# Scores of the local attention from high and low parts of queries and keys, in three float32r products

## The reference, cut to what matters

```python
def swa_sink_mixer(h, w_in, b_in, sinks, w_out, b_out):
    proj = h @ w_in + b_in
    q, k, v = jnp.split(proj, [...], axis=-1)
    ...
    s = jnp.einsum('bnqkgd,bnskd->bnkgqs', q, kb) * (SWA_HEAD_DIM ** -0.5)
    ...
    mx = jnp.maximum(jnp.max(s, axis=-1, keepdims=True), sink)
    e = jnp.exp(s - mx)
    p = e / (jnp.sum(e, axis=-1, keepdims=True) + jnp.exp(sink - mx))
    o = jnp.einsum('bnkgqs,bnskd->bnqkgd', p.astype(vb.dtype), vb)
    return o.reshape(B, T, SWA_Q_HEADS * SWA_HEAD_DIM) @ w_out + b_out
```

## Time and profile before

| | us |
|---|---|
| median of three runs | 1897.83 (1897.42 to 1898.5) |
| the profiled execution's own time | 1897.43 |
| its span in the profile | 1895.6 |
| TensorE busy, of the span | 1888.5 |
| VectorE busy | 1344.0 |
| ScalarE busy | 987.4 |
| full float32 score matmuls of the local attention | 128 instructions, first at 586.0, last at 651.5 |

### The profile page before, as it was taken

The page is one execution under the profiler, slowest core; times in us unless marked ns, Lnnn a source line. Parts: engine busy times, 40 slices in busy tenths (PEclk is TensorE's granted clock), DMA queues, the critical chain, the costliest instruction groups (busy, mean ns, idle before and its releaser), DMA issues. The chain is left out here.

```text
span 1895.6 us, 25342 instructions
## 1 busy us (share of the span) xinstructions
PE 1888.5 (100%) x9432; PEld 1554.5 (82%) x9432; DVE 1344.0 (71%) x2000; ACT 987.4 (52%) x1591; POOL 96.1 (5%) x114
## 2 busy tenths in 40 slices
PE   9999999999999999999999999999999999999999
PEld 8877888888888788888888988667788888888887
DVE  8656665556566766665666788998897877767867
ACT  5634464454546756454544335788435455545454
POOL 0100000101000000000100000000000000100101
PEclk9999999999999999999999999999999999999999
DMA  7632156758323124766742346232234634654735
GB/s 232 157 100 100 66 152 174 168 161 216 119 67 143 45 67 131 192 147 176 178 154 68 122 134 170 87 94 73 90 96 138 167 89 156 157 149 116 199 96 122
DMA packets 70684, 249.79 MB, mean 132 GB/s; under 512 B 7970, under 2 KB 8226, under 8 KB 69924
## 3 DMA queue, kind: packets, MB, share of 16 engines
q1 hardware_dynamic: 56448, 198.82, 31.2%
q0 software_dynamic: 13824, 49.29, 15.1%
q10 hardware_dynamic: 292, 0.07, 0.0%
HBM read 246.05 MB, written 2.10 MB: 131 GB/s over the span
## 5 line engine op out<-in xcount | busy, mean ns | idle before, releaser
L553 PE MATMUL ps<-HH,WH 128*128 128x512 f32 (+1 forms) x1676 | 623.4, 372 | 0.0
L555 PE MATMUL ps<-HH,WL 128*128 128x512 f32 (+1 forms) x1676 | 618.4, 369 | 0.0
L554 PE MATMUL ps<-HL,WH 128*128 128x512 f32 (+1 forms) x1676 | 618.2, 369 | 0.0
L1346 ACT ACTIVATE WH<-WR 128x1024 fp32r<-128x1024 f32 x331 | 346.9, 1056 | 473.3 <-PE ps L555 308.9
L2109 DVE TENSOR_TENSOR WL<-WR,WH 128x1024 fp32r<-128x1024 f32 x330 | 400.7, 1219 | 260.0 <-ACT WH L1346 259.3
L553 PEld LDWEIGHTS ps<-HH,WH 128*128 128x128 f32 x1676 | 316.2, 189 | 62.3 <-issue 10.0
L555 PEld LDWEIGHTS ps<-HH,WL 128*128 128x128 f32 x1676 | 316.2, 189 | 53.0
L554 PEld LDWEIGHTS ps<-HL,WH 128*128 128x128 f32 x1676 | 316.3, 189 | 51.2
L1006 PE MATMUL ps<-WL,AH 128*128 128x512 f32 x490 | 190.9, 390 | 0.0
L1005 PE MATMUL ps<-WH,AL 128*128 128x512 f32 x490 | 190.8, 389 | 0.0
L1004 PE MATMUL ps<-WH,AH 128*128 128x512 f32 x490 | 190.8, 389 | 0.0
(11 more groups left out here) (401 smaller groups left out, 2616.0 us busy)
## 6 DMA issues: line engine op xcount, KB each, us to landing
WR<-in_up SPq DMA_DIRECT2D x96, 512.0 KB, 4.4
WR<-in_quart SPq DMA_DIRECT2D x60, 512.0 KB, 3.5
WR<-in_quart POOLq DMA_DIRECT2D x48, 512.0 KB, 6.4
WR<-in_in SPq DMA_DIRECT2D x48, 512.0 KB, 3.5
WR<-in_down SPq DMA_DIRECT2D x16, 512.0 KB, 3.5
WR<-in_quartf SPq DMA_DIRECT2D x14, 512.0 KB, 3.5
WR<-in_quartf POOLq DMA_DIRECT2D x14, 512.0 KB, 5.7
MT<-in_up SPq DMA_DIRECT2D x12, 512.0 KB, 3.8
```

The lines of the kernel that those rows point to most:

```text
L553: e.matmul(ps, wh, hi[:, c, cols], start=c == 0 and not (shared and h), stop=False, skip_group_check=shared)
L554: e.matmul(ps, wh, lo[:, c, cols], start=False, stop=False, skip_group_check=shared)
L555: y = e.matmul(ps, wl, hi[:, c, cols], start=False, stop=c == x.n - 1, skip_group_check=shared)
L1346: e.activation(x.wh[:, 0:n], raw(m, x.raw)[:, 0:n], AF.Copy).then_inc(*k.mark("whi", u))
```

## The change

The scores are no longer one product of `WQ` and `WK` in full float32. ScalarE copies keys and each query pair to float32r (`WKH`, `WQH`, the latter with two buffers), VectorE subtracts these from the float32 values (`WKL`, and `WQL`, which lie over `WK` and `WQ`), and TensorE adds three float32r products in PSUM for each block and head: high query x high key, high query x low key, low query x high key. `score(p)` waits for the low parts instead of the evacuations.

```diff
     def score(p):
-        e.wait_ge(*k.on("ae", u + 2 + p))
-        e.wait_ge(*k.on("ae", u))
+        e.wait_ge(*k.on("hlo", "q", p))
+        e.wait_ge(*k.on("hlo", "k"))
+        qh, ql = m.WQH[:, p % 2, :], m.WQL[:, p, :]
...
-                for s in range(2):
-                    b, half = SWA_BANKS[g][s], slice(64 * s, 64 * s + 64)
-                    x = e.matmul(ps[b][:, f:f + n], m.WQ[half, p, blk * 128:(blk + 1) * 128], m.WK[half, k0:k0 + n],
-                                 start=True, stop=True)
+                for j, (query, key) in enumerate(((qh, m.WKH), (qh, m.WKL), (ql, m.WKH))):
+                    for s in range(2):
+                        b, half = SWA_BANKS[g][s], slice(64 * s, 64 * s + 64)
+                        x = e.matmul(ps[b][:, f:f + n], query[half, blk * 128:(blk + 1) * 128], key[half, k0:k0 + n],
+                                     start=j == 0, stop=j == 2)
...
     def evac(j):      # ScalarE
         if j == 0:
             e.activation(m.WK[:, :], p, AF.Identity, bias=par(m, "swa_bk")).then_inc(*k.mark("ae", u + j))
+            e.wait_ge(*k.on("ae", u + j))
+            e.activation(m.WKH[:, :], m.WK[:, :], AF.Copy).then_inc(*k.mark("hhi", "k"))
...
+            e.wait_ge(*k.on("ae", u + j))
+            if j > 3:
+                e.wait_ge(*k.on("score", "w", 2 * j - 7, 1))
+            e.activation(m.WQH[:, j % 2, :], m.WQ[:, j - 2, :], AF.Copy).then_inc(*k.mark("hhi", "q", j - 2))
...
+    def low_q(p):     # VectorE
+        e.wait_ge(*k.on("hhi", "q", p))
+        e.tensor_tensor(m.WQL[:, p, :], m.WQ[:, p, :], m.WQH[:, p % 2, :].bitcast(F32), A.subtract).then_inc(
+            *k.mark("hlo", "q", p))
+
     for j in range(1, 5):
         v_cut(e, k, u + j + 3)
+        if j == 1:
+            e.wait_ge(*k.on("hhi", "k"))
+            e.tensor_tensor(m.WKL[:, :], m.WK[:, :], m.WKH[:, :].bitcast(F32), A.subtract).then_inc(*k.mark("hlo", "k"))
+        elif j > 2:
+            low_q(j - 3)
     for p in range(8):
         score(2 * p)
         score(2 * p + 1)
...
         weigh(2 * p + 1)
+        if p < 6:
+            low_q(p + 2)
```

More of the change, by code:

```diff
@@ L341, in memory @@
     m.WQ = arena("WQ", [128, 8, T], 0)
+    m.WQL = arena("WQL", [128, 8, T], 0, F32R)
+    m.WKL = over("WKL", [128, T], acc, F32R)
+    m.WKH = over("WKH", [128, T], dg + 2 * KB, F32R)
+    m.WQH = over("WQH", [128, 2, T], tmp, F32R)
     m.PW = arena("PW", [128, 4, 896], 16)
@@ L1072, in score @@
                 k0, n = SWA_KEYS[blk]
-                for s in range(2):
-                    b, half = SWA_BANKS[g][s], slice(64 * s, 64 * s + 64)
-                    x = e.matmul(ps[b][:, f:f + n], m.WQ[half, p, blk * 128:(blk + 1) * 128], m.WK[half, k0:k0 + n],
-                                 start=True, stop=True)
-                    if blk == group[-1]:
-                        x.then_inc(*k.mark("score", "w", 2 * p + s, g))
-                        k.free[b] = ("smax", "w", 2 * p + s, g)
+                for j, (query, key) in enumerate(((qh, m.WKH), (qh, m.WKL), (ql, m.WKH))):
[3 more added lines that the diff above has]
+                                     start=j == 0, stop=j == 2)
+                        if blk == group[-1] and j == 2:
+                            x.then_inc(*k.mark("score", "w", 2 * p + s, g))
+                            k.free[b] = ("smax", "w", 2 * p + s, g)
                 f += n
```

## The result

The changed kernel takes 1900.5 us, median of 22 runs (1899.3 to 1902.6); the kernel before 1897.6 (22 runs, 1897.2 to 1898.5). The ratio is 1.0015, interval 1.0009 to 1.0021: 2.9 us slower, a small but measured loss. The prediction was 1899.8 in 1896.8 to 1902.5, no change leaning to slower. The scatter is part of the result. Sorted by the mean TensorE clock of the whole execution, the 22 runs are two groups: eleven from 1899.3 to 1900.3 with a clock of 1.000, and eleven from 1900.7 to 1902.6 with 0.999 or 0.998. The median of the first group is 2.3 us above before, that of the second 3.8. The times alone leave only 0.3 us between the groups, so it is the clock that divides them. The profiled execution, 1901.25 around a span of 1899.4, is one of the second.

What follows compares the result with a forecast made beforehand. TensorE, busy 1888.5 of 1895.6 us, was taken as the bound, with waits at out(0) and out(5) deciding. Terms +1.84 - 0.33 + 0.595 gave +2.1 us, so 1899.8 us, range 1896.8 to 1902.5.

Steps and rivals of the forecast that it cites:

- TensorE's own work: Score calls: 1.62 us against 1.72, about 0.11 less per call, 0.9 us for all eight.
- B: Rival in the score calls: float32r halves don't run side by side; +8.7 us, 1906.5; chance 0.13.
- C: Rival in the score calls: 128 columns of float32r cost as much as full float32; +3.4 us, 1901.2; chance 0.15.
- ScalarE and VectorE, per pair: Added work per query pair: ScalarE's copy delays what follows by 0.675 us, VectorE's subtraction by 0.595.
- The start: Before 586 us (keys, pairs 0 and 1): added work hidden; otherwise score(0) at most 1.3 us later.
- Place 1: Iterations 0 and 1 up to out(0): one chain without idle time makes out(0) wait, all behind it +1.84 us.
- Middle iterations: Iterations 3 to 5: added work ends in idle time, TensorE saves 0.11 us in each, 0.33 in all.
- Place 2: Up to out(5): VectorE's subtraction in the chain from turn(9) adds 0.595 us; scores 6 and 7 save nothing.
- The sum: Whole kernel: +1.84 - 0.33 + 0.595 = +2.1 us, forecast 1899.8 us.
- D: Rival: added work covered at one or both places in iterations 0 and 1 or later; 1897.2 with both covered; chance 0.12.

Runs made afterwards that it cites:

- the reordered heads: Changed kernel with each block's three products of one head, then three of the other, in program order: 1899.71 us, ratio 1.0005 to 1.0023.
- the pause filled: Changed kernel plus ten float32r matmuls in front of out(0), their result overwritten later: 1899.56 us, ratio 1.0000 to 1.0017.
- the long one: Kernel before plus 3.9 us of unread ScalarE copies ahead of the first copy of turn(1): 1903.44 us, ratio 1.0020 to 1.0044.
- the best version: Changed kernel with copies and subtractions moved into idle time and ScalarE's first turn(2p - 1) copy ahead of evac(p + 4): 1896.63 us, ratio 0.9986 to 1.0004.

## Why the prediction was right, and where it wasn't

- **TensorE's own work**: right. A call takes 1.61 us, predicted 1.62; pairs side by side, steps 0.12 and 0.11. B (halves one after the other) and C (128 columns as dear as full float32) fell by the rows of `score(0)`. In the middle each call gives 0.10 to 0.13, where 0.11 was predicted.
- **ScalarE and VectorE, per pair**: right. The copy takes 0.63 with 0.04 ahead of it, the subtraction 0.69; moving each engine's work by itself gave 1.3 for two copies and 0.6 for one subtraction.
- **The start**: hidden, as said; `score(0)` starts 0.09 later than before, and the same 0.09 is there at 560 us, ahead of the added work.
- **Place 1**: right in place and size, +1.89 for the copy's end against +1.84, `out(0)` 4.52 us with the clock kept against 4.6. That its saving in three scores is waited away is right too.
- **Middle iterations**: right, no wait for ScalarE or the low parts in iterations 3 to 5.
- **Place 2**: size right (+0.61 by VectorE's copies, 0.595 predicted), place partly wrong. I followed VectorE to `out(5)`; TensorE stops earlier, at `turn(11)`, for ScalarE's copies of `turn(10)`, which hang in the same chain. `out(5)` grew by 0.13, not 0.8.
- **The sum**: +2.1, and that is what undisturbed executions show: +2.03 in the profile of the reordered heads, +2.1 with the pause filled, and the eleven faster runs of the change +1.7 to +2.7.
- **What was missed**: the price of the pause beyond its length. The prediction made TensorE's wait in `out(0)` 1.84 us longer or so and charged it once. In about half of the executions, by times and clocks, the clock falls to the lower level behind it, and the work there costs 1.2 us more in `out(0)` and 0.45 in the product behind it, 1.6 in all. Half of that and the +2.1 make the 2.9, and it is most of the scatter. The sum of the terms lacked this one. That the median still lies in the range is in part luck: its upper end was drawn for C, which did not happen.
- **D** (the added work covered) fell for the kernel as it is, but its price came out: with the work moved so that it is covered at both places the time is 1897.05, D's was 1897.2. Where the copies and subtractions stand decides, more than the products.

Shown: both places, by moving each engine's work alone; the fall of the clock behind the pause in two profiles of the change, and by a pause alone, the long one. Argued from times: that filling the pause keeps the clock up. Open: what decides in which executions a pause of 2.2 us lets the clock fall, since the profile of the reordered heads has the pause without the fall; whether a pause of that length without the change does it; what the two high runs with the filled pause had; and whether the best version beats the kernel before.

## What to carry to other kernels

Where the bounding engine is near 100% busy, what counts is not how much work goes to the others but where it stands in their order: put it just ahead of a wait of theirs, and follow each chain to the instruction at which the bounding engine will stand still. A pause of 2.2 us on TensorE cost its length here and in some executions 1.6 us more, when the clock fell behind it; read the granted clock in windows just after every pause, since the busy share hides it. Time saved on TensorE in front of a wait for another engine was worth nothing here, so ask of each saving which wait comes next.

## What the runs showed of the hardware beside that

Float32r matmuls on 64 rows each ran in pairs, one on each half of the 128 rows, even when the program has three of one half and then three of the other (starts 10 ns apart, call 1.61 us in either order). By the steps of such pairs, three float32r products cost 0.36 us where one full float32 product costs 0.43 for 256 columns, but 0.33 against 0.22 for 128 columns. After a pause of 4.1 us the one profile shows the clock fall, and all six runs have a mean clock of 0.999 or 0.998. After one of 2.2 us two of three profiles show it, and after one of 1.9 neither of two.
